# An unused block of 16 in place of 96 floats in front of the normed activations

## The chip, the core and the metric

The kernel runs on one core of a Trainium2 chip. The metric is the device time of one execution in microseconds (us). Three runs of the kernel before gave 1245.01, 1246.52 and 1247.16 us; their median, 1246.52 us, is what the change is measured against.

## What is computed

Two transformer-like stacks in a row on one sequence of 256 tokens of 1024 features, all in float32. What carries the time are matrix products of the normed activations with large weight matrices:

```python
def conv_glu_ffn(h, w_up, conv_w, conv_b, w_down):
    z = h @ w_up
    ...
    return (jax.nn.silu(gate) * val) @ w_down
def swiglu(h, w_gate_up, w_down):
    g, u = jnp.split(h @ w_gate_up, 2, axis=-1)
    return (jax.nn.silu(g) * u) @ w_down
```

The first stack has a layer with a gated recurrence (an input projection of 2816 columns, an output projection) and a layer with attention, each followed by the first kind of feed-forward network (FFN, 1024 to 5632 and 2816 to 1024). The second stack has a layer with attention and one with a short convolution, each followed by the second kind of FFN. Each of the second stack's norms is scaled and shifted by a vector that comes from `silu(c) @ w_ada` (two matrices of 1024 x 6144). Eight RMS norms stand in front of the eight blocks; the last norm is at the end of the first stack.

## The kernel before

The 256 tokens stay on the chip. All weights stream in once from HBM. The DMA queue of SyncE loads them in chunks of 1 or 2 MB into two ring buffers (`ring0`, `ring1`, line 486). Each chunk is split into halves of 128 x 2048 floats, and each half into two float32r parts, so that three fast products give one float32 product: ScalarE rounds the half into `whi` (`split_hi`, L618) and VectorE writes the rest into `wlo` (`split_lo`, L624). There are four buffers of each (lines 487 and 488). The normed activations are split in the same way, transposed, into a high and a low part: `hhi`, `hlo` (`HT0`, line 505) for the first norm alone and `ghi`, `glo` (`HT1`, line 511) for the seven others. Each part is 128 x 2048 floats, 8 blocks of 256 tokens, one for each 128 features. `ht(k)` (line 522) gives the pair of norm k.

TensorE uses them in four ways:

- `pe_tile` (L1081 to L1083): 128 columns of weights stand in the array, and 256 floats of activations move past them. Three products for each of 8 blocks, twice: 48 products for a tile. The up projections, the queries and keys and the convolution's input projection are made of these.
- `pe_first` (L848 to L850): the first two tiles behind a norm, with the parts exchanged: 128 tokens of activations stand and 256 floats of weights move. It begins as soon as the first 128 tokens are normed. Its results are turned back in `pe_turn_back` (L882), behind the first half of the next tile.
- `pe_rows` (L1096 to L1098): the same exchanged parts, for values and for some keys.
- `pe_sum_part` (L1110): the down and output projections. The operand that stands is `yhi` or `ylo` (line 491), and 512 floats of `whi` or `wlo` move. Neither lies behind the block that is changed.

The instructions that load what stands in the array are LDWEIGHTS (PEld in the profile); they run beside the products, one load for one product. In the order written by hand in `walk`, `OD` and `MO`, VectorE also works through `w_ada` (L2219, L2222) in steps between its other work, from a part of `arena` into which SyncE's queue loads it.

On-chip memory is given out as a stack, in the order of the lines 486 to 517, the same number of bytes in each of the 128 partitions. In front of the block `gap_h` (line 502, used by nobody) lie the ring, the split weights, `x`, `xn`, `yhi`, `ylo`, the constants, small vectors and `ada`. Behind it lie everything whose life ends early (`mix`, `h`, `pre`, `solve`, lines 504 to 510) and, over the same bytes, `ghi`, `glo`, `arena`, `gates`, `acc`, `att`, `rows` and `mgain` (lines 511 to 517):

```python
        AHI, ALO = (sb(f"ada{i}", 512, F32R)[:, :] for i in ("hi", "lo"))
        sb("gap_h", 96)
        MIX, PRE, SOLVE = ExitStack(), ExitStack(), ExitStack()
        RW = part(MIX, "mix", 32 * 256)
        HT0 = [c3(part(PRE, f"h{i}", NK * T, F32R)[:, :], NK) for i in ("hi", "lo")]
        ...
        HT1 = [c3(part(ctx, f"g{i}", NK * T, F32R)[:, :], NK) for i in ("hi", "lo")]
        AR = part(ctx, "arena", 36 * 256)
```

The products of a tile (L1076 to L1083):

```python
                    c = (8 * a + k) * 128 if pair else 256 * k + 128 * a
                    wh, wl = hi[:, c:c + 128], lo[:, c:c + 128]
                    e.matmul(o, wh, h[0][:, k, :], start=k == 0, stop=False)
                    e.matmul(o, wh, h[1][:, k, :], start=False, stop=False)
                    x = e.matmul(o, wl, h[0][:, k, :], start=False, stop=k == NK - 1)
```

All blocks in front of the changed one and behind it have sizes such that every one of these slices begins, within 256 bytes, where its buffer begins: the steps are 512 or 1024 bytes.

The stages, by their start in the profile: the recurrence's layer from 0, its FFN 0 from about 164 us, queries, keys and attention from 353, FFN 1 from 468, the second stack's attention from 657, FFN 2 from 771, the convolution from 961, FFN 3 from 1053 us to the end.

## Time and profile before

| | |
|---|---|
| median of 3 runs | 1246.52 us |
| the profiled execution's own time | 1246.01 us |
| its span, first to last instruction | 1244.2 us |
| TensorE busy (products) | 98% of the span |
| VectorE, ScalarE, GpSimd busy | 75%, 56%, 2% |
| granted TensorE clock | full, from the first slice to the last |
| read from HBM | 261.43 MB, 211 GB/s over the span |

An engine's busy time is the union of its instructions. A product's recorded duration reaches over its pipeline and overlaps the next ones, so 281 ns is not what a product costs: that is the distance from one start to the next, read from the timeline.

### The profile page before, as it was taken

To read this page: it belongs to the slowest core of one execution; us is meant where nothing else is said; L and a number is where in the kernel's file an instruction comes from. 1 tells how busy PE (TensorE), PEld (TensorE's weight loads), DVE (VectorE), ACT (ScalarE), POOL (GpSimd) and SP (SyncE) were. 2 spreads that over 40 slices of the span, in tenths; PEclk is the share of its full clock that TensorE was granted. 3 is DMA by queue.
4 is the path that set the end of the run, shared out by engine and by line. 5 is a ranking of instruction groups with operands and counts; after the bars stand their busy time and mean duration, and the time that the engine had idled before them with its cause. 6 is when DMAs were issued, how large, how long until landed. Compare 5 with 4: busy or idle time off the path is not lost.

```text
span 1244.2 us, 23631 instructions
## 1 busy us (share of the span) xinstructions
PE 1221.6 (98%) x9983; PEld 1140.4 (92%) x9983; DVE 932.5 (75%) x1259; ACT 702.0 (56%) x1030; POOL 29.5 (2%) x34
## 2 busy tenths in 40 slices
PE   6999999999999999999999999999999999999998
PEld 6999899999899879999989998999998998999997
DVE  5897379888769777999977567799986676666553
ACT  6843477655565667656567556634445555643432
POOL 0041000000000000000000000000000000000000
PEclk9999999999999999999999999999999999999999
DMA  9550287776667256789663534799975456775550
GB/s 323 179 204 4 74 267 237 270 244 202 223 211 266 75 187 219 228 299 320 237 217 107 197 125 152 253 359 346 352 282 203 137 206 201 248 251 180 202 170 34
DMA packets 163825, 264.04 MB, mean 212 GB/s; under 512 B 5692, under 2 KB 98056, under 8 KB 163720
## 3 DMA queue, kind: packets, MB, share of 16 engines
q1 hardware_dynamic: 160728, 259.80, 60.8%
q10 hardware_dynamic: 2992, 2.72, 0.8%
q8 instruction: 79, 1.29, 0.4%
q14 instruction: 26, 0.21, 0.1%
HBM read 261.43 MB, written 1.05 MB: 211 GB/s over the span
## 4 chain that ended last, share of the span: by engine, by line
PE 89%; DVE 5%; DMA 3%; issue 2%; ACT 1%; SPq 0%; ACTq 0%; DVEq 0%
PE ps L1110 24%; PE ps L1081 15%; PE ps L1082 15%; PE ps L1083 15%; DVE acc L2222 2%; PE ps L1096 2%; DVE wlo L624 2%; PE ps L1098 2%; PE ps L1097 2%; PE ps L848 2%; PE ps L849 2%; PE ps L850 2%; PE ps L2398 2%; DMA arena<-in_w_ada_dram 2%; PE ps L828 1%
## 5 line engine op out<-in xcount | busy, mean ns | idle before, releaser
L624 DVE TENSOR_TENSOR wlo<-ring,whi 128x2048 fp32r<-128x2048 f32 x194 | 443.2, 2288 | 94.6 <-ACT whi L618 94.3
L1081 PE MATMUL ps<-ghi,whi 128*128 128x256 f32 x1600 | 449.1, 281 | 0.2 <-DVE gates L2241 0.2
L1083 PE MATMUL ps<-ghi,wlo 128*128 128x256 f32 x1600 | 447.5, 280 | 0.0
L1082 PE MATMUL ps<-glo,whi 128*128 128x256 f32 x1600 | 447.5, 280 | 0.0
L618 ACT ACTIVATE whi<-ring 128x2048 fp32r<-128x2048 f32 x194 | 370.6, 1914 | 126.5 <-PE ps L1110 58.6
L1081 PEld LDWEIGHTS ps<-ghi,whi 128*128 128x128 f32 x1600 | 301.6, 189 | 2.6 <-issue 1.2
L1083 PEld LDWEIGHTS ps<-ghi,wlo 128*128 128x128 f32 x1600 | 303.8, 190 | 0.0
L1082 PEld LDWEIGHTS ps<-glo,whi 128*128 128x128 f32 x1600 | 300.7, 188 | 0.8
L1110 PE MATMUL ps<-whi,yhi 128*128 128x512 f32 x480 | 159.5, 396 | 0.7 <-DVE ylo L2000 0.7
L1110 PE MATMUL ps<-wlo,yhi 128*128 128x512 f32 x480 | 156.6, 390 | 0.0
L1110 PE MATMUL ps<-whi,ylo 128*128 128x512 f32 x480 | 156.5, 390 | 0.0
L1110 PEld LDWEIGHTS ps<-whi,ylo 128*128 128x128 f32 x480 | 90.1, 188 | 19.0
L1110 PEld LDWEIGHTS ps<-wlo,yhi 128*128 128x128 f32 x480 | 90.2, 188 | 18.6
L1110 PEld LDWEIGHTS ps<-whi,yhi 128*128 128x128 f32 x480 | 88.2, 188 | 20.1 <-issue 2.2
L2222 DVE SCALAR_TENSOR_TENSOR acc<-arena,small,acc 128x512 f32<-128x512 f32 x126 | 94.6, 751 | 6.5 <-DMA arena<-in_w_ada_dram 2.6
L2259 DVE SCALAR_TENSOR_TENSOR arena<-arena,cols 128x254 f32<-128x254 f32 (+1 forms) x176 | 73.8, 479 | 14.7 <-ACT arena L1772 14.1
L2274 DVE TENSOR_TENSOR ylo<-arena,yhi 128x256 fp32r<-128x256 f32 x88 | 37.1, 422 | 48.3 <-ACT yhi L1789 48.2
L848 PE MATMUL ps<-whi,ghi 128*128 128x256 f32 x224 | 63.4, 283 | 3.9 <-DVE glo L994 3.9
L1770 ACT ACTIVATE arena<-ps 128x512 f32<-128x512 f32 x44 | 26.3, 598 | 65.8 <-PE ps L1083 63.8
L849 PE MATMUL ps<-wlo,ghi 128*128 128x256 f32 x224 | 62.6, 280 | 0.0
L850 PE MATMUL ps<-whi,glo 128*128 128x256 f32 x224 | 62.6, 279 | 0.0
L1776 ACT ACTIVATE arena<-ps 128x256 f32<-128x256 f32 x44 | 16.7, 379 | 80.6 <-PE ps L1083 80.5
(312 smaller groups left out, 1573.4 us busy)
## 6 DMA issues: line engine op xcount, KB each, us to landing
arena<-in_w_ada_dram SPq DMA_DIRECT2D x48, 1024.0 KB, 6.5
ring<-in_ff_w_up_dram SPq DMA_DIRECT2D x44, 1024.0 KB, 7.6
ring<-in_w_gate_up_dram SPq DMA_DIRECT2D x44, 1024.0 KB, 7.6
ring<-in_ff_w_down_dram SPq DMA_DIRECT2D x10, 2048.0 KB, 7.9
ring<-in_w_down_dram SPq DMA_DIRECT2D x10, 2048.0 KB, 7.8
ring<-in_od_w_qkv_dram SPq DMA_DIRECT2D x6, 2048.0 KB, 8.4
ring<-in_w_qkv_dram SPq DMA_DIRECT2D x6, 2048.0 KB, 8.0
ring<-in_w_in_dram SPq DMA_DIRECT2D x6, 2048.0 KB, 8.0
```

Source lines behind the costliest of these rows:

```text
L618: e.activation(shaped(WHI[i % NB], k), v, ACT.Copy).then_inc(S["w_hi"], 1)
L624: e.tensor_tensor(shaped(WLO[i % NB], k), v, shaped(WHI[i % NB], k).bitcast(F32), ALU.subtract).then_inc(S["w_lo"], 1)
L848: e.matmul(o, h[0][:, c, t], wh, start=c == 0, stop=False)
L849: e.matmul(o, h[0][:, c, t], wl, start=False, stop=False)
L850: x = e.matmul(o, h[1][:, c, t], wh, start=False, stop=c == NK - 1)
L1081: e.matmul(o, wh, h[0][:, k, :], start=k == 0, stop=False)
L1082: e.matmul(o, wh, h[1][:, k, :], start=False, stop=False)
L1083: x = e.matmul(o, wl, h[0][:, k, :], start=False, stop=k == NK - 1)
L1110: x = e.matmul(ps[:, :], YT[l][:, src_k + i, t], w[r][:, i, 512 * h:512 * h + 512], start=first, stop=last)
L2222: e.scalar_tensor_tensor(a, AW[:, k, :], SC[:, k:k + 1], a, ALU.mult, ALU.add).then_inc(S["ada_acc"], 1)
L2259: e.scalar_tensor_tensor(t[a][:, lag:256], z[:, 256 * a:256 * a + 256 - lag], conv_col(f, 2 - lag, a * NF + p), t[a][:, lag:256], ALU.mult ...
L2274: e.tensor_tensor(YT[1][:, p % 8, :], tg[r], YT[0][:, p % 8, :].bitcast(F32), ALU.subtract).then_inc(S["y_lo"], 1)
```

## The change

The unused block in front of the activations shrinks from 96 to 16 floats in each partition, 384 to 64 bytes. Everything that is allocated behind it moves down by 320 bytes. `hhi`, `hlo`, `ghi`, `glo`, `arena` and the blocks up to `att` then begin at a multiple of 256 bytes. `whi` and `wlo` stay where they are, 128 bytes behind a multiple of 256. No instruction, wait or queue changes.

```diff
@@ -499,7 +499,7 @@
         NORM.close()
 
         AHI, ALO = (sb(f"ada{i}", 512, F32R)[:, :] for i in ("hi", "lo"))
-        sb("gap_h", 96)
+        sb("gap_h", 16)
         MIX, PRE, SOLVE = ExitStack(), ExitStack(), ExitStack()
         RW = part(MIX, "mix", 32 * 256)
         HT0 = [c3(part(PRE, f"h{i}", NK * T, F32R)[:, :], NK) for i in ("hi", "lo")]
```

Of the kernel before, what the change touches and what calls it, by code (L numbers as in the profile page):

```python
# [456 lines left out]
def program(nc, A, consts, out):  # L457
    with ExitStack() as ctx:
        def sb(name, cols, dt=F32, rows=128):
            return ctx.enter_context(nc.sbuf_tensor(name, [rows, cols], dt))  # L460
# [38 lines left out]
        NORM.close()  # L499

        AHI, ALO = (sb(f"ada{i}", 512, F32R)[:, :] for i in ("hi", "lo"))
        sb("gap_h", 96)
        MIX, PRE, SOLVE = ExitStack(), ExitStack(), ExitStack()
        RW = part(MIX, "mix", 32 * 256)
        HT0 = [c3(part(PRE, f"h{i}", NK * T, F32R)[:, :], NK) for i in ("hi", "lo")]
# [2260 lines left out]
```

## Rows read from the trace of the kernel before

**Rows 1.** The page: busy time by engine, and the clock in 40 slices (9: full)
```profile
PE 1221.6 (98%) x9983; PEld 1140.4 (92%) x9983; DVE 932.5 (75%) x1259; ACT 702.0 (56%) x1030; POOL 29.5 (2%) x34
...
PEclk9999999999999999999999999999999999999999
```
**Rows 2.** The page: the chain that ended last, shares by engine
```profile
PE 89%; DVE 5%; DMA 3%; issue 2%; ACT 1%; SPq 0%; ACTq 0%; DVEq 0%
```
**Rows 3.** Waits of TensorE's products, longest: total us, times, longest us
```profile
PE ps L802 <- DMA pre<-in_ev_norm_dram: 5.0, 1, 5.0
PE ps L848 <- DVE glo L994: 3.9, 4, 1.5
```
**Rows 4.** The timeline, TensorE: ends of 80 triples (L1081 to L1083), FFN 0
```profile
182.94 0.28 PE L1081 MATMUL ps<-ghi,whi 128*128 128x256 f32 x1
...
210.85 0.28 PE L1081 MATMUL ps<-ghi,whi 128*128 128x256 f32 x1
```
**Rows 5.** The timeline, TensorE: ends of 144 triples, the convolution's input projection
```profile
979.93 0.28 PE L1081 MATMUL ps<-ghi,whi 128*128 128x256 f32 x1
...
1028.55 0.28 PE L1081 MATMUL ps<-ghi,whi 128*128 128x256 f32 x1
```
**Rows 6.** Line 1081 in those two stretches: durations ns min/median/max, first and last start
```profile
L1081 PE MATMUL ps<-ghi,whi x80: 280/281/282, 182.9 to 210.9; 128*128 128x256 f32 x80
...
L1081 PE MATMUL ps<-ghi,whi x144: 276/276/277, 979.9 to 1028.6; 128*128 128x256 f32 x144
```
**Rows 7.** Groups of weight loads, 180 to 211 us: count, busy us, mean ns
```profile
L1081 PEld LDWEIGHTS ps<-ghi,whi 128*128 128x128 f32 x88 | 16.9, 192 | 0.0
L1082 PEld LDWEIGHTS ps<-glo,whi 128*128 128x128 f32 x88 | 16.5, 188 | 0.0
```
**Rows 8.** Line 1081: the span (page), 783 to 1053 us, and four stretches
```profile
L1081 PE MATMUL ps<-ghi,whi 128*128 128x256 f32 x1600 | 449.1, 281 | 0.2 <-DVE gates L2241 0.2
...
L1081 PE MATMUL ps<-ghi,whi x480: 275/276/387, 783.3 to 1028.6; 128*128 128x256 f32 x160
...
L1081 PE MATMUL ps<-ghi,whi x88: 276/276/367, 484.1 to 513.8; 128*128 128x256 f32 x88
...
L1081 PE MATMUL ps<-ghi,whi x88: 275/276/367, 786.9 to 816.6; 128*128 128x256 f32 x88
L1081 PE MATMUL ps<-ghi,whi x64: 276/276/387, 828.9 to 851.0; 128*128 128x256 f32 x64
L1081 PE MATMUL ps<-ghi,whi x160: 276/276/367, 973.6 to 1028.6; 128*128 128x256 f32 x160
```
**Rows 9.** Products with standing activations: L848 (224 triples), L1096 (160), over the span
```profile
L848 PE MATMUL ps<-whi,ghi x224: 276/279/365, 163.9 to 1065.1; 128*128 128x256 f32 x112
...
L1096 PE MATMUL ps<-whi,ghi x160: 276/279/467, 403.3 to 740.7; 128*128 128x256 f32 x160
```
**Rows 10.** The chain in order of time: 48 products of 512 floats (L1110)
```profile
1168.27 10.88 PE ps L1110 x48
```
**Rows 11.** Line 1081 with `hhi`, recurrence's layer: two stretches
```profile
L1081 PE MATMUL ps<-hhi,whi x32: 281/281/282, 50.9 to 61.8; 128*128 128x256 f32 x32
...
L1081 PE MATMUL ps<-hhi,whi x65: 276/276/684, 61.8 to 87.6; 128*128 128x256 f32 x65
```
**Rows 12.** Busy us by engine, clock, DMA share and GB/s in three stretches
```profile
783.00:884.00 101.00, 100.79 (x794) 95.08 (x793) 89.30 (x104) 46.91 (x54) 0.00 (x0) 1.00 0.95 331
884.00:957.00 73.00, 73.00 (x474) 66.76 (x474) 57.95 (x67) 33.29 (x37) 0.00 (x0) 1.00 0.80 279
1065.00:1240.00 175.00, 175.00 (x1242) 164.44 (x1240) 101.24 (x100) 73.01 (x79) 0.00 (x0) 1.00 0.54 184
```
**Rows 13.** DMA issues: count, KB each, median us to landing
```profile
arena<-in_w_ada_dram SPq DMA_DIRECT2D x48, 1024.0 KB, 6.5
ring<-in_ff_w_up_dram SPq DMA_DIRECT2D x44, 1024.0 KB, 7.6
```
**Rows 14.** Waits of VectorE, 784 to 884 us: total us, times, longest
```profile
DVE acc L2222 <- DMA arena<-in_w_ada_dram: 2.6, 2, 1.5
```

## The prediction

> **What bounds the kernel now.** I read the page first: TensorE's products cover 98% of the span at the full granted clock, its upper level of 2.4 GHz, in every slice [rows 1]. The chain that ended last says the same in another way: 89% of it are TensorE's [rows 2]. The waits agree: the longest of them are 5.0 us at the very start and 3.9 us in four waits behind norms [rows 3]. So the time is the number of products times the distance from one start to the next, and the change can only matter through that distance.
>
> The timeline shows that distance, and there are two values for the same line. In FFN 0, line 1081 starts at 182.94 and, 79 triples of products later, at 210.85 [rows 4]: 27.91 us / 237 = 117.8 ns. In the convolution's input projection it takes from 979.93 to 1028.55 for 143 triples [rows 5]: 48.62 / 429 = 113.3 ns. The reader should see that this is no jitter: within each stretch the recorded durations are alike to 2 ns, 281 in the one and 276 in the other [rows 6], so the duration tells the pace of a stretch at a glance. In the slow pace one of the three weight loads takes 192 ns and another 188 [rows 7]. It is a lock of two streams, the load of the next block and the block that moves, which run beside each other.
>
> **How much stands in each pace.** Of 1600 triples with `ghi` [rows 8] the long stretches with 276 ns hold 88 + 88 + 64 + 160 = 400 [rows 8]; going through the rest stretch by stretch I found 56 more in five short ones. That leaves 1144 slow triples, 3432 products, and 456 fast ones, 1368 products. Products with standing activations are 224 triples at line 848 and 160 at line 1096, median 279 ns where the lowest is 276 [rows 9]; I read 276 as the fast pace there, take the same step between the two, and count the 224 as slow and at most 160 more. The 512-float products are 10.88 us / 48 = 226.7 ns apart [rows 10], twice 113.3, so they are at the fast pace already, and neither of their operands moves.
>
> **The change part by part.** It adds and removes no instruction, DMA or wait. Sizes give the places: 96 floats are 384 bytes, 16 are 64, so all that lies behind goes down by 320 bytes. It ends at a multiple of 256, so it was 64 behind one. The split weights are 128 behind one, before and after. The distance between the two streams of a tile's product goes from 64 to 128 bytes, modulo 256.
>
> *The tile products (L1081 to L1083).* No row shows them at the new distance. The bounds come from the two paces that the trace has, 117.8 - 113.3 = 4.43 ns apart before rounding. All fast: 3432 x 4.43 = -15.2 us. All slow: 1368 x 4.43 = +6.1 us. What sets the pace is not the distance alone, since at one distance both occur: with `hhi`, which lies as `ghi` does modulo 256, 32 triples are slow and the next ones fast [rows 11]. It changes where the stream is broken, behind a norm or between rows and tiles, and holds until the next break. So I take the distance as one of the things that decide into which pace a break leads. Between the bounds I take the best mixed part that the trace has, 783 to 1053 us, with two breaks behind norms and several between rows and tiles: 480 triples [rows 8], of them 88 + 64 + 160 = 312 fast, 65%. If the whole kernel had that share, 0.35 x 1600 = 560 triples would be slow in place of 1144, and 584 x 3 x 4.43 = -7.8 us. That is nearer to the middle than to an end, and I choose it because the recorded breaks lead to either side.
>
> *Standing activations (L848, L1096).* Bounds: all fast, (224 + 160) x 3 x 4.43 = -5.1 us; slower, +2.1 us if the 160 are fast today and go slow. The median of line 848 over seven stages is the slow duration [rows 9], through different breaks, so I take 0.
>
> *The 512-float products, transposes, VectorE, ScalarE.* The first have no moved operand: 0. VectorE's and ScalarE's work on `arena`, `gates` and `acc` moves with them by 320 bytes. It stands behind TensorE: VectorE is busy 89.30 of 101 us in the tightest stretch and 101.24 of 175 in FFN 3 [rows 12]. 0, with the cover gone only if it grew by a tenth.
>
> *The loads of `w_ada` into `arena`.* They end at new places too. 1 MB lands in 6.5 us there, 64 behind a multiple of 256, and in 7.6 us in the ring, 128 behind one [rows 13]; VectorE waited 2.6 us for them where DMA was busiest [rows 14], TensorE not at all. Bounds 0 and, if those waits went and TensorE could use it, -2.6 us; I take 0. [...]
>
> *What would be late next.* In FFN 2 faster tiles would ask for weights sooner: DMA share 0.95 and VectorE 88% busy up to 884 us, 0.80 and 79% behind [rows 12]. Of 168 slow triples between 783 and 1053 only some 64 lie ahead of 884, so at most 64 x 3 x 4.43 = 0.9 us of the all-fast gain could come back as waits.
>
> Sum: -7.8 us on an execution of 1246.01 us (span 1244.2, 1.8 us around it). It stands 0.5 us below the median of 1246.52, so on the median 1238.7 us.
>
> **The rivals.** *No effect (about 1246.5).* The pace may hang on how the two streams meet in time, on instruction fetch or on the order of breaks, and not on where they read. For: both paces exist at one distance [rows 6, 11], and the fast one is reached at a distance of 64. Against: the runs of before agree within 2.2 us though 4.43 ns on all tile products would be 21 us, so the breaks lead to the same pace each time, and something fixed decides it. The Trainium skill ("SBUF — State Buffer", "SBUF: two separate sides") gives TensorE a port of its own, with a second independent read port for weight loads, and says that slow-downs come from structural stalls alone; by that rule a shift of 64 bytes is worth nothing. Rows 7 show a load 4 ns longer at one of three places, which neither confirms nor excludes it.
>
> *Slower: the fast stretches lock slow.* Place: the 88 triples from 484.1, 88 from 786.9, 64 from 828.9 and 160 from 973.6 [rows 8]. If at the new distance each break ends in the slow pace, they cost 4.43 ns more for each product: 400 x 3 x 4.43 = 5.3 us, with the short ones 6.1, and with line 1096 up to 8.2: 1252.6, at most 1254.7. It decides from the point where more triples turn slow than fast; within 2.5 us it cannot be told from no effect, which is 190 triples of balance. For it: the fast pace is the rarer one, 456 of 1600.
>
> *Slower by a worse lock.* If not one but all three loads of a triple were held up, each by what the one costs a triple, 3 x 4.43 = 13.3 ns, a product would be 126.6 ns from the next: 8.9 ns on 3432 and 13.3 on 1368 products, 30.5 + 18.2 = +49 us. No stretch shows such a pace.
>
> *Faster: the slow pace goes altogether.* -15.2 - 5.1 = -20.3: 1226.2. For it: a slow load in each third place looks like two streams that ask for the same thing, and a distance of half of 256 bytes keeps them farthest apart. This is the far end of the forecast's own case.
>
> **How the numbers follow.** Forecast (share of slow triples falls, by anything from 3 to 20 us): 0.50, of which the far end, below 1229, has about 0.1. No effect: 0.21. Fast stretches turn slow: 0.25, nearly all of it 3 to 8 us above. Worse lock: 0.04. A difference of 0.2%, 2.5 us, is about what a measurement of this kernel can tell from none. So faster 0.50, same 0.21, slower 0.29. Forecast and slower hold most of the chance with opposite signs: the forecast's own range is 1228 to 1243. The range for all, 1227 to 1255, leaves out the worse lock, the last microsecond of the far end, and some of the slower case's upper part, some 0.15 in all.
>
> **What would show it.** Right: in the changed kernel more stretches of line 1081 with 276 ns between starts 113.3 ns apart, the weight loads of all three lines at 188, the 512-float products still 226.7, granted clock full, waits of TensorE as before. The saving should be 13.3 ns times the triples that changed sides; if the count does not give the time, the reason is wrong even if the time is right. Wrong: a median of 281 in the same stretches as before (no effect), the stretches of [rows 8] at 281 (slower), a third duration (worse lock or a new one), or a change of time that sits in waits, in VectorE's instructions or in landing times.

## The result and the profile after

The changed kernel takes 1263.34 us (median of 4 runs, 1262.53 to 1263.84) against 1245.76 us before (4 runs, 1244.64 to 1247.16): a ratio of 1.014, 95% interval 1.0122 to 1.0157. It is slower by 17.6 us, beyond the end of the predicted range. The profiled execution took 1263.84 us, with a span of 1262.0.

The page of the changed kernel, engines, clock and the chain's shares:

```profile
PE 1239.1 (98%) x9983; PEld 1157.6 (92%) x9983; DVE 933.2 (74%) x1259; ACT 703.0 (56%) x1030; POOL 28.2 (2%) x34
...
PEclk9999999999999999999999999999999999999999
...
PE 97%; DVE 1%; ACT 1%; issue 1%; DMA 1%; SPq 0%; DVEq 0%; ACTq 0%
```

Beside [rows 1, 2]: the same number of instructions at the same full clock, VectorE within 0.7 us and ScalarE within 1.0, and TensorE busy for 17.5 us more. That is the whole loss of 17.6 us, and it is not made of waits. The waits of TensorE's products are as in [rows 3]:

```profile
PE ps L802 <- DMA pre<-in_ev_norm_dram: 5.1, 1, 5.1
PE ps L848 <- DVE glo L994: 4.0, 4, 1.5
```

So the products are farther apart. The view of line 1081 in single stretches (durations min/median/max in ns, first and last start), first the two stretches that were fast before [rows 8, 5], FFN 1's first tiles and the convolution, then FFN 3's, then the exchanged products (line 848, to compare with [rows 9]):

```profile
L1081 PE MATMUL ps<-ghi,whi x88: 282/287/362, 490.3 to 521.7; 128*128 128x256 f32 x88
...
L1081 PE MATMUL ps<-ghi,whi x152: 282/287/362, 990.2 to 1044.7; 128*128 128x256 f32 x152
...
L1081 PE MATMUL ps<-ghi,whi x88: 279/281/364, 1085.3 to 1116.4; 128*128 128x256 f32 x88
...
L848 PE MATMUL ps<-whi,ghi x224: 279/281/367, 167.1 to 1081.3; 128*128 128x256 f32 x112
```

The first runs from 490.3 to 521.7 where it ran from 484.1 to 513.8: 31.4 us in place of 29.7 for 87 triples, 120.3 ns for a product in place of 113.7 (each with one gap of 0.2 us inside, without which it is 120.0 and 113.4; the distances are from the starts before rounding). The convolution's is 120.2 ns; before, the products of its 143 triples stood 113.3 apart. FFN 3's is 119.0 ns, 118.6 without its gap. No stretch at 113.3 is left. In their place are paces of 118.3 to 120.0 ns without gaps, all above the slow one of before, and most products are at one of two, 118.6 and 120.0. The weight loads of the first of these stretches are no longer 192, 188, 188 as in [rows 7] or all 188, but all alike and longer:

```profile
L1081 PEld LDWEIGHTS ps<-ghi,whi 128*128 128x128 f32 x88 | 16.8, 190 | 0.0
L1083 PEld LDWEIGHTS ps<-ghi,wlo 128*128 128x128 f32 x88 | 16.8, 190 | 0.0
L1082 PEld LDWEIGHTS ps<-glo,whi 128*128 128x128 f32 x88 | 16.8, 190 | 0.0
```

That is so in the stretches at 120.0 alone. In those at 118.6, as FFN 0's first tiles, the mean of all three groups is 188 ns, as in the fast pace of before.

The 512-float products, of which no operand moved, keep their pace of [rows 10]:

```profile
1185.32 10.89 PE ps L1110 x48
```

I averaged the distance from each start to the next over each trace, where a product follows at once. The tiles went from 116.4 to 119.3 ns, lines 848 to 850 from 117.6 to 118.9, lines 1096 to 1098 from 116.7 to 118.8, line 1110 from 227.3 to 227.6. Times 5232, 672, 576 and 1440 products that is 15.2 + 0.9 + 1.2 + 0.4 = 17.7 us.

### The profile page after: what moved, and what is told of

It reads as the page before. It is cut to its first block, busy times and chain, and to the rows that moved or that the text cites. A ratio compares the mean times of both kernels' runs of the same rounds, so it can differ in the third digit from the quotient of the medians.

```text
span 1262.0 us, 23631 instructions
## 1 busy us (share of the span) xinstructions
PE 1239.1 (98%) x9983; PEld 1157.6 (92%) x9983; DVE 933.2 (74%) x1259; ACT 703.0 (56%) x1030; POOL 28.2 (2%) x34
## 4 chain that ended last, share of the span: by engine, by line
PE 97%; DVE 1%; ACT 1%; issue 1%; DMA 1%; SPq 0%; DVEq 0%; ACTq 0%
PE ps L1110 25%; PE ps L1081 17%; PE ps L1083 17%; PE ps L1082 17%; PE ps L848 2%; PE ps L850 2%; PE ps L849 2%; PE ps L1096 2%; PE ps L1098 2%; PE ps L1097 2%; PE ps L2398 2%; PE ps L828 1%; DMA ring<-in_ev_w_in_dram 1%; PE ps L2407 1%; PE ps L2598 1%
## 5 line engine op out<-in xcount | busy, mean ns | idle before, releaser
L1083 PE MATMUL ps<-ghi,wlo 128*128 128x256 f32 x1600 | 453.1, 283 | 0.0
L1081 PE MATMUL ps<-ghi,whi 128*128 128x256 f32 x1600 | 452.6, 283 | 0.0
L1082 PE MATMUL ps<-glo,whi 128*128 128x256 f32 x1600 | 452.5, 283 | 0.0
L1081 PEld LDWEIGHTS ps<-ghi,whi 128*128 128x128 f32 x1600 | 302.6, 189 | 2.0 <-issue 1.2
L1083 PEld LDWEIGHTS ps<-ghi,wlo 128*128 128x128 f32 x1600 | 302.2, 189 | 0.0
L1110 PE MATMUL ps<-whi,yhi 128*128 128x512 f32 x480 | 159.7, 396 | 0.7 <-DVE ylo L2000 0.7
L1110 PE MATMUL ps<-wlo,yhi 128*128 128x512 f32 x480 | 156.6, 390 | 0.0
L1110 PE MATMUL ps<-whi,ylo 128*128 128x512 f32 x480 | 156.6, 390 | 0.0
L1110 PEld LDWEIGHTS ps<-whi,ylo 128*128 128x128 f32 x480 | 90.1, 188 | 19.2
L1110 PEld LDWEIGHTS ps<-wlo,yhi 128*128 128x128 f32 x480 | 90.1, 188 | 18.8
L1110 PEld LDWEIGHTS ps<-whi,yhi 128*128 128x128 f32 x480 | 88.2, 188 | 20.3 <-issue 2.6
L848 PE MATMUL ps<-whi,ghi 128*128 128x256 f32 x224 | 64.0, 286 | 4.0 <-DVE glo L994 4.0
```

The source lines that it names most:

```text
L848: e.matmul(o, h[0][:, c, t], wh, start=c == 0, stop=False)
L1110: x = e.matmul(ps[:, :], YT[l][:, src_k + i, t], w[r][:, i, 512 * h:512 * h + 512], start=first, stop=last)
```

## The experiments

The theory (D in the expectations): the distance between the moving and the standing operand of a product, modulo 256 bytes, decides how fast products can follow one another. The first rival (P): it is the place of the activations that counts, whatever the weights. The second (A): the loss comes from the other things that moved. All times are medians; each comparison is with the kernel before on the same chip (1244.66 to 1246.87 us).

**The same place 256 bytes lower.**

```diff
-        sb("gap_h", 96)
+        sb("gap_h", 32)
```

> The unused block has 32 floats: the activations begin 64 bytes behind a multiple of 256, as before the change, but 256 bytes lower than before. Theory D (the distance between the operand that moves and the one that stands, modulo 256 bytes, sets the pace): the old pace mix of 113.3 and 117.8 ns comes back, 1246 us within 3. Rival P (the place of the activations modulo 256 counts, whatever the weights): the same, 1246. Rival F (the pace hangs on something finer or wider, as the distance modulo 512 bytes, which differs from both kernels): another mix, anywhere from 1226 to 1263 us.

1247.0 us, ratio 1.0004 (0.9995 to 1.0013). The time is back, with the two old paces. Neither the theory nor the first rival falls; going down by 256 bytes alone changed nothing.

**Activations at a multiple of 256, weights moved with them.**

```diff
+        sb("gap_w", 48)
         WHI = [sb(f"whi{i}", HALF, F32R)[:, :] for i in range(NB)]
...
-        sb("gap_h", 96)
+        sb("gap_h", 32)
```

> A block of 48 floats ahead of the split weights and one of 32 ahead of the activations: the activations begin at a multiple of 256 bytes, as in the changed kernel, and the split weights 64 behind one, so the distance between them is that of the kernel before. Theory D: line 1081 back to 113.3 and 117.8 ns, 1246 us. Rival P: no product at 113.3, paces of 119 to 120.2 ns, 1263 us. This run tells D from P.

1245.94 us, ratio 1.0002 (0.9993 to 1.0011). The activations begin at a multiple of 256 bytes, as in the changed kernel, and nothing is lost. The convolution's stretch, line 1082 of this kernel:

```profile
L1082 PE MATMUL ps<-ghi,whi x152: 276/276/367, 978.5 to 1030.0; 128*128 128x256 f32 x152
```

276 ns, and 51.5 us where the changed kernel took 54.5. The first rival is out: it is the distance. Of the distances, 64 below is the only one that was tried at two places within 256 bytes.

**The rest of memory, each way.** First the changed kernel with all behind the activations at its old addresses, then the kernel before with only that part at a multiple of 256:

```diff
-        sb("gap_h", 96)
+        sb("gap_h", 16)
...
+        part(ctx, "gap_a", 80)
         AR = part(ctx, "arena", 36 * 256)
```

> The changed kernel, with an unused block of 80 floats behind the activations, so that arena, gates, acc and all behind them have their old addresses to the byte; only the activations (ghi, glo, and hhi, hlo, mix, pre, solve of the first layer) stay moved. Theory D (the distance between the two operands of a product): nothing comes back, 1263 us. Rival A (part of the loss is in VectorE's, ScalarE's and the DMAs' accesses to the moved arena, which reach TensorE as interference): a part comes back, below 1260 us.

1263.72 us, ratio 1.014 (1.0125 to 1.0155): nothing comes back.

```diff
+        part(ctx, "gap_a", 48)
         AR = part(ctx, "arena", 36 * 256)
```

> The kernel before, with an unused block of 48 floats behind the activations: the activations keep their addresses, arena and all behind it begin at a multiple of 256 bytes, as in the changed kernel. Theory D: 1246 us. Rival A: slower by over 3 us. If loads into the arena at a multiple of 256 bytes land faster, their median comes down from 6.5 us.

1246.38 us, ratio 1.0009 (0.9999 to 1.0018), so at most 2.2 us, and no effect is within the interval. The second rival is out. The landings of `w_ada` went from 6.5 us [rows 13] to 5.9 in the changed kernel, but to 6.3 in both of these runs, of which one has the arena at a multiple of 256 and the other has not:

```profile
arena<-in_w_ada_dram SPq DMA_DIRECT2D x48, 1024.0 KB, 6.3
```

**Other distances.** The block alone, with 0, 48, 24, 40, 36, 28, 56 and 8 floats. Two of the expectations name places that their kernels do not have: each block begins at a multiple of 32 bytes, so 36 floats (144 bytes) take the room of 40, and 28 floats (112 bytes) that of 32. In the programs as built `ghi` begins at byte 149600 of a partition with 36 floats as with 40, and at 149568 with 28 as with 32.

> No unused block: the activations begin 192 bytes behind a multiple of 256, 64 above the split weights in place of 64 below. Theory D, if only the size of the distance counts: 1246 us; if the sign counts, the paces of moving and standing activations exchange, since line 848 has moved weights 64 above the activations today: line 1081 then mostly at 117.8 ns, 1252 us. Rival P: only a multiple of 256 is bad, so 1246.

> The unused block has 48 floats: activations and split weights begin at the same place modulo 256 bytes. Theory D: distance 0 is a case of its own; if the two streams ask for the same part of the memory at the same time it is the worst, 120 ns or more for a product, 1263 us or above; if the hold-up at 128 came from the reading at twice the speed that catches up in mid-way, it is the best, all products at 113.3 ns, 1226 us. Rival P: 128 behind a multiple is as good as 64, so 1246.

> The unused block has 24 floats: the activations begin 32 bytes behind a multiple of 256, 96 below the split weights. Theory D with whole parts of 64 bytes (the operands ask for the same part or not): a block that begins in mid-part shares time with two parts, so something between 1246 and 1263 us. Theory D with a finer grain: a pace that no run has shown so far. If the place within a part is of no matter, 1246 or 1263 as its neighbours.

> The unused block has 40 floats: the activations begin 96 bytes behind a multiple of 256, 32 below the split weights. Theory D in parts of 64 bytes: between 1246 and 1268 us, and the mirror of a distance of 96 below if the pattern repeats each 128 bytes, so about the time of that run. With a finer grain: a pace of its own, faster ones not excluded.

> The unused block has 36 floats: the activations begin 80 bytes behind a multiple of 256, 48 below the split weights, between the place of before (64 below) and that of the run with 40 floats (32 below, 1256.96 us). If the loss grows with the distance from 64, about 1251 us; if lines of 16 bytes are all alike, 1246; if 64 below is not the best place but only one next to it, faster than 1246.

> The unused block has 28 floats: the activations begin 48 bytes behind a multiple of 256, 80 below the split weights, between 96 below (1260.43 us) and 64 below (1246). 48 below and 32 below came out alike (1256.72 and 1256.96). If reads are counted in units of 32 bytes and a start in mid-unit counts as the next unit, 80 below is as 64 below: 1246 us. If any start off a multiple of 64 bytes is bad, or a start in mid-unit counts as the unit before, it is as 96 below: 1260 us.

> The unused block has 56 floats: the activations begin 160 bytes behind a multiple of 256, 32 above the split weights, an untried unit of 32 bytes. If the units mirror around distance 0, as 32 below: 1257 us. If what is above is a milder case of what is below, as 64 above was 1251 against 1246, 1251 to 1262.

> The unused block has 8 floats: the activations begin 224 bytes behind a multiple of 256, 96 above the split weights, the last untried unit of 32 bytes. Mirror of 96 below: 1260 us; if the best place of all were here, tiles mostly at 113.3 ns and 1230 us.

What they gave, by the place of the activations behind a multiple of 256 bytes (the weights are at 128). The pace is that of the convolution's 152 triples, first to last start, which holds one gap of a fraction of a microsecond:

| place | block, floats | distance | time, us | ratio to before (95%) | pace, ns |
|---|---|---|---|---|---|
| 0 (the change) | 16 | 128 | 1263.34 | 1.014 (1.0122 to 1.0157) | 120.2 |
| 32 | 24 | 96 below | 1260.43 | 1.0111 (1.0095 to 1.0126) | 118.8 |
| 64 (before) | 96 | 64 below | 1245.76 | | 113.6 |
| 64 | 32 | 64 below | 1247.0 | 1.0004 (0.9995 to 1.0013) | 113.6 |
| 64 | 28 | 64 below | 1244.91 | 0.9996 (0.9985 to 1.0006) | 113.6 |
| 96 | 40 | 32 below | 1256.96 | 1.0087 (1.007 to 1.0104) | 118.5 |
| 96 | 36 | 32 below | 1256.72 | 1.0082 (1.0067 to 1.0097) | 118.5 |
| 128 | 48 | 0 | 1267.83 | 1.0173 (1.0158 to 1.0188) | 120.2 |
| 160 | 56 | 32 above | 1249.27 | 1.0018 (1.0007 to 1.0028) | 116.9 |
| 192 | 0 | 64 above | 1251.09 | 1.0038 (1.0024 to 1.0052) | 118.0 |
| 224 | 8 | 96 above | 1266.01 | 1.0157 (1.0136 to 1.0177) | 120.2 |

The pace of one stretch is not the whole of a place. At place 64 this one ran at 118.0 ns in two of the other kernels, the one with the arena alone moved and the one with `yhi` and `ylo` moved. At place 0, in the kernel with the arena at its old addresses, it ran at 118.8:

```profile
L1082 PE MATMUL ps<-ghi,whi x152: 279/281/364, 989.5 to 1043.3; 128*128 128x256 f32 x152
```

With 56 and with 8 floats the time fell outside everything that was expected (1251 to 1262, and 1260 or 1230). The rows of line 1081 behind two of the places. Place 128, distance 0:

```profile
L1081 PE MATMUL ps<-ghi,whi x152: 283/283/362, 993.9 to 1048.3; 128*128 128x256 f32 x152
```

Place 160, which is 32 above:

```profile
L1081 PE MATMUL ps<-ghi,whi x152: 277/280/366, 980.6 to 1033.5; 128*128 128x256 f32 x152
```

A recorded duration does not give the pace across places: the convolution's 120.2 ns come with a median of 287 at place 0 and of 283 at place 128. Three things follow. The longest time is that of distance 0, with 96 above so near that their intervals overlap. At distance 0 all three weight loads (groups of the same stretch, mean in ns) take the 192 ns that one in three took before:

```profile
L1083 PEld LDWEIGHTS ps<-ghi,wlo 128*128 128x128 f32 x153 | 29.4, 192 | 0.0
L1082 PEld LDWEIGHTS ps<-glo,whi 128*128 128x128 f32 x152 | 29.2, 192 | 0.0
L1081 PEld LDWEIGHTS ps<-ghi,whi 128*128 128x128 f32 x152 | 29.2, 192 | 0.0
```

Longer loads do not make the pace, though. In the same stretch at place 160 all three groups are at 188 ns, as in the fast pace of before, and the products stand 116.7 ns apart without the gap:

```profile
L1081 PEld LDWEIGHTS ps<-ghi,whi 128*128 128x128 f32 x152 | 28.6, 188 | 0.0
L1083 PEld LDWEIGHTS ps<-ghi,wlo 128*128 128x128 f32 x151 | 28.4, 188 | 0.0
```

How fine the grain is stays open: no place between the multiples of 32 bytes was measured, and the pairs with one place are repeats that agree within 2.1 us. And the sign counts: 64 above costs 5 us over 64 below, though lines 1095 to 1097 of that kernel, whose moving operand is then 64 below the standing one, went to the fast pace (median 276 ns in place of 279 in [rows 9]):

```profile
L1095 PE MATMUL ps<-whi,ghi x160: 276/276/469, 404.2 to 741.5; 128*128 128x256 f32 x160
```

Where 64 below is the good distance, it is so for either operand that moves.

**Which operands meet.** A load runs beside the product ahead of it. To tell the operands of one product from these neighbours in time, parts of the split were moved alone.

```diff
-        HT1 = [c3(part(ctx, f"g{i}", NK * T, F32R)[:, :], NK) for i in ("hi", "lo")]
+        HT1 = [c3(part(ctx, "ghi", NK * T, F32R)[:, :], NK)]
+        part(ctx, "gap_g", 16)
+        HT1.append(c3(part(ctx, "glo", NK * T, F32R)[:, :], NK))
```

> The kernel before, with an unused block of 16 floats between ghi and glo: glo alone goes up by 64 bytes, to the place of the split weights modulo 256, ghi keeps its own. One product in three (line 1082 in a tile) then moves an operand at distance 0. If each hold-up belongs to one product, a third of what the run with all at distance 0 showed comes: tiles at about 117.6 ns on average in place of 116.4, some 1252 us. If any bad product locks all, 1263 us or above; if only a majority counts, 1246.

1252.92 us, ratio 1.0051 (1.0034 to 1.0068), tiles at 117.6 ns on average, as expected if each hold-up belongs to one product. But the sum comes out in another way: no stretch with `ghi` is at the fast pace any more. Seven in eight of their products are at 117.8, the slow pace of before, and the rest at 119.2. The end of the fast pace alone is worth 1368 x 4.43 = 6.1 us. One moved product in a triple was enough for that. Within a triple the next start comes 119.8 ns after line 1082's product, whose `glo` moved, and 117.6 and 116.5 after the other two (average over all triples with `ghi`). For the next kernel `glo` is moved as here, and `wlo` as well:

```diff
+        sb("gap_l", 16)
         WLO = [sb(f"wlo{i}", HALF, F32R)[:, :] for i in range(NB)]
+        sb("gap_m", 48)
...
-        sb("gap_h", 96)
+        sb("gap_h", 32)
```

> glo goes up by 64 bytes and so does wlo (blocks of 16 and 48 floats around wlo, 32 in front of the activations, so that all else keeps its place modulo 256). The operands of one product are then at distance 0 (glo with whi) or 128 (ghi with wlo) in two of three. But the load that runs beside a product is that of the next one: beside moving glo runs the load of wlo, beside moving ghi that of whi, and all these pairs are 64 below, as before. Theory N (neighbours in time meet): 1246 us. Theory O (the two operands of one product meet): two of three products bad, about 1260 us.

1262.01 us, ratio 1.0127 (1.0112 to 1.0142). Tiles at 118.5 ns on average, worse than with `glo` alone, though each product and the load recorded beside it are at the old distance. The neighbours' theory (N), which expected 1246 us, does not hold by itself. It is not shown false with that: from one product to the next both the moving and the standing operand now alternate by 64 bytes, and no run has this alternation without a bad distance. Some 11 of the 16 us are the tiles' (5232 x 2.1 ns); the rest is in the 512-float products, which was not expected:

```profile
1182.57 11.12 PE ps L1114 x48
```

231.7 ns each in place of 226.7. The next kernel keeps the three lines around `wlo` and leaves `ghi` and `glo` together:

> wlo alone goes up by 64 bytes (blocks of 16 and 48 floats around it, 32 in front of the activations). In the tiles the moving operands ghi and glo keep their common place, and one load in three (wlo, with moving ghi) comes to a distance of 128. In the 512-float products the moving operands whi and wlo now alternate by 64. Theory D alone: tiles at 117.4 to 117.8 ns on average in place of 116.4 to 117.1, and the 512-float products at 227.3. Theory M (it hurts too when moving operands alternate by 64 bytes, whatever stands): the 512-float products at 231 ns as with glo and wlo moved, 5 to 6 us. If M is all that slowed the run with glo alone, the tiles stay at 117.1 or below.

1260.72 us, ratio 1.0115 (1.0099 to 1.0132). Tiles at 118.2 ns, above the 117.4 to 117.8 that one product in three at distance 128 was to cost. The moving operands do not alternate here, so their alternation is not needed for a loss; the standing ones, `whi` and `wlo`, still do. Nor is the hold-up where the theory of a product's own operands would have it: the next start comes 116.2 ns after line 1083's product (in the kernel before the change), the only one whose own operands are at 128, and 119.0 and 119.5 after those of lines 1081 and 1082. The 512-float products stay at 230.8 ns, as theory M expected (it hurts when moving operands alternate by 64 bytes).

Then `yhi` and `ylo` alone are moved:

```diff
+        sb("gap_y", 48)
         YT = [c3(sb(f"y{i}", NK * T, F32R)[:, :], NK) for i in ("hi", "lo")]
+        sb("gap_z", 16)
...
-        sb("gap_h", 96)
+        sb("gap_h", 32)
```

> yhi and ylo alone move (a block of 48 floats in front of them, 16 behind): the 512-float products of line 1110 then have their moving weights 64 above the operand that stands, in place of at distance 0; tiles keep 64 below. If these products are indifferent, since a weight load takes only half of their time, 226.7 ns and 1246 us. If what raised them from 227.3 to 231.3 ns on average in the run with glo and wlo moved is their distance (there one in three had 64 above), all of them now rise by up to 12 ns: 1440 x 12 ns = 17 us, up to 1263 us.

1244.66 us, ratio 0.9992 (0.998 to 1.0003). The time says indifferent, the trace does not: the 512-float products rose to 229.7 ns on average,

```profile
1167.96 11.01 PE ps L1112 x48
```

which is 1440 x 2.4 = 3.5 us, and the tiles fell to 115.8 ns from 116.4, about 3.0 us, because more of their stretches ran in the fast pace. A time alone would have hidden this. Chance in the one traced execution does not explain it well, since the median of ten executions is that of before too; whether the place of `yhi` and `ylo` makes the fast pace more frequent is open. So the distance of the 512-float products matters as well, less, and for them 0 is better than 64. When only `wlo` is 64 above, they lose more than when both are, so something beyond the distance of one product's operands acts on them; theory M names one candidate, alternation, and no run isolates it.

**The kernel before, once more.**

> The kernel before once more, unchanged, for its trace. If something fixed in the program decides which stretches of line 1081 are fast, the same 456 of 1600 triples are at 113.3 ns, in the same stretches. If the timing at each break decides (landing of DMAs, clocks of the engines), the stretches differ from those of the first trace while the paces themselves, 113.3 and 117.8, stay.

1246.63 us. Two stretches of the second trace, FFN 1's and FFN 2's first tiles:

```profile
L1081 PE MATMUL ps<-ghi,whi x88: 281/281/363, 484.0 to 514.9; 128*128 128x256 f32 x88
...
L1081 PE MATMUL ps<-ghi,whi x88: 276/276/367, 788.0 to 817.7; 128*128 128x256 f32 x88
```

In [rows 8] both were fast; now the first is slow, by 1.2 us. In the kernel with a block of 32 floats FFN 0's first tiles were fast (180.3 to 210.0 us, median 276) and FFN 2's slow. So which stretches are fast is not fixed by the program, and the paces stay. A few such draws at 1.2 to 2 us each are as large as the spread of the runs.

No version beat the kernel before; those that keep its distance in the tiles' products, 64 below in all of them, are equal to it.

## Why the prediction was wrong

**What bounds the kernel** held: TensorE's products, at distances that do not come from waits. The whole change of time was in them. That nothing else would matter held too: VectorE, ScalarE and the loads were costed at 0, and the two runs on the arena confirm it, within 2.2 us.

**The step that failed** is the bounds of the tile products: "The bounds come from the two paces that the trace has". Both paces belong to one distance, 64 below; they are what a break can lead to there. A new distance has paces of its own: at 128 they run from 118.3 to 120.0 ns and average 119.3, above the upper bound of 117.8. All stretches, slow and fast, went to them: 5232 x 2.9 ns = 15.2 us, where the forecast had -7.8 and the lower and upper ends -15.2 and +6.1. Two smaller terms failed with it. The sum counts only the products with `ghi` and leaves out the 432 with `hhi`, which move as well and went from 114.6 to 119.0 ns, 1.9 of the 15.2 us. The products with standing activations were put at 0 and cost 0.9 + 1.2 us.

**The share of fast stretches** was worked out as if the distance set it by degrees, from a mixed part of the trace. The share at the old distance is not fixed, as the second trace shows, and at the new one it is zero. The sentence against "no effect", that "the breaks lead to the same pace each time", was wrong as well: a spread of 2.2 us leaves room for stretches of 1.2 us that change sides, and one of the two compared here did.

**The rivals.** The worse lock came nearest, with the right sign, products slower than any seen before, and a chance of 0.04. Its mechanism, a hold-up of all three loads of a triple, is seen in part: at place 0 they are longer in the stretches at 120.0 ns and not in those at 118.6. Its price was too high: it took the whole 13.3 ns for each load and came to +49 us. At distance 0 all three loads are at 192 ns, and the distance between starts is 120.0 ns there, 6.7 more than the fast pace and not 13.3: a triple with three such loads takes 20 ns more, one with one such load 13. With that, 3432 x 2.2 + 1368 x 6.7 = 16.7 us for the tiles with `ghi` would have been its price. The reason for the far end, that half of 256 bytes keeps the streams farthest apart, is refuted: 128 is nearly as bad as 0 (1263.34 and 1267.83 us).

**The lock.** The prediction took it for one between the load of the next block and the block that moves. With `glo` and `wlo` both moved, these pairs kept their old distance and 16 us were lost all the same, so that cannot be all of it.

**What was read in the notes.** The Trainium skill ("SBUF — State Buffer", "SBUF: two separate sides") gives the weight loads a second independent read port. By that the shift would have been worth nothing. The runs differ by up to 22 us for nothing but a distance, so the measurement decides against its use here. The Trainium skill ("DMA: Bandwidth & Descriptors", "How a descriptor splits into AXI transactions") lets a descriptor that does not start at a multiple of 256 bytes begin with a transaction from the boundary below, whose unused bytes cost beats. No run here shows it for the place that is written: the landings took 6.3 us with and without the multiple of 256.

**What stays open** is why. The runs show which distances between the activations and the split weights are good, in steps of 32 bytes. They do not show what the two share, nor which load and which product have to be kept apart: the kernels that move `glo` or `wlo` alone mix distance with alternation. Nor can a product and its own load be told from a product and the load before its own, or the load of the product two places later: in a triple these are the same pairs of buffers.

## What to carry to other kernels

With 128 columns standing and 256 floats moving for each product, the place of the two buffers relative to each other was worth up to 1.7% of this kernel, which is bound by TensorE, for no instruction at all. Read the distance between starts in the timeline before believing a bound, and if it is above the best stretch of the trace, try the place of one buffer in steps of 32 bytes over 256. Here 64 bytes below was the one good distance of eight, and the tidy choices, 0 and 128, were among the bad ones. Look up where a block really begins: a step smaller than the unit in which blocks are placed changes nothing. A pace seen in a trace bounds only the arrangement that it was seen in.

## What was not expected of the hardware

- Eight places within 256 bytes gave 1244.91 to 1267.83 us with identical instructions; the three kernels at one of them, place 64, gave 1244.91 to 1247.0. 64 below and 64 above differ (1245.76 and 1251.09 us), and so do 32 below and 32 above (1256.96 and 1249.27).
- At 64 below, two paces of 113.3 and 117.8 ns exist side by side; a stretch keeps its own from one break to the next, and which it gets differed between two executions of the same program. At 128 there are again two that hold most products, 118.6 and 120.0 ns, and the convolution's stretch had one in the changed kernel and the other in the one with the arena moved back.
- The recorded length of the weight loads does not follow the pace: all three are at 188 ns at paces of 113.3, 116.7 and 118.6 ns, and at 192 at 120.0.
- 512-float products, whose loads are recorded at 188 ns, are not free of it: from 227.3 to 229.7 ns on average when the standing operand was moved by 64 bytes, and to 230.8 and 231.3 ns when one of the moving ones was.
